# Attention with 64-wide values: values as the stationary operand, outputs born turned

## The chip, the cores and the metric

The kernel runs on one core of a Trainium2 chip. It is one program for the whole forward pass, and its time is the device time of one execution, in microseconds. The engines of the core are TensorE (PE in the rows; PEld are its weight loads), VectorE (DVE), ScalarE (ACT), GpSimd (POOL) and SyncE (SP), which issues most DMAs. Each has its own queue, worked in order; they meet only through semaphores.

## The reference

Two layers of one kind (latent attention, mLSTM and SSD mixers, then routed experts) are followed by two layers of a second kind. Only these second layers are changed. Each computes, for 512 tokens of width 1024:

```python
h = rms_norm(x, attn_norm_g[l])
proj = h @ w_in[l]
(mq, mk, mv, dq, dk, dv, sq, sk, sv, iq, ik, iw) = jnp.split(proj, offsets, axis=-1)
moba = moba_attention(...)          # 4 heads, values 64 wide
...
a = probs(q1, k1) - lam * probs(q2, k2)         # differential: 4 heads, values 128 wide
diff = rms_norm(diff, diff_subln_g[l]) * (1.0 - lam_init)
dsa = dsa_attention(...)            # 4 heads, values 64 wide, top 128 keys by the indexer
mix = jnp.concatenate([merge_heads(moba), merge_heads(diff), merge_heads(dsa)], axis=-1)
x = x + mix @ w_out[l]
h2 = rms_norm(x, ffn_norm_g[l])
x = x + (jax.nn.silu(h2 @ w_gate[l]) * (h2 @ w_up[l])) @ w_down[l]
```

All three attentions are causal softmaxes over tiles of 128 queries. The order of the rows of `w_out` and of the columns of `mix` may be chosen freely as long as both agree.

## The kernel before

A dense product with float32 accuracy is made of three matmuls: each operand is split into a high part (a copy rounded by ScalarE) and a low part (the difference, by VectorE or GpSimd), and `product` (lines 264 to 266) multiplies high by high, low by high and high by low. Weights come in units of 128x2048 through `WeightStream`: SyncE loads a unit into one of three raw slots, ScalarE makes its high part (L215), VectorE or GpSimd the low part (L253), and TensorE may use it once `lo_ready` has counted it. A raw slot is loaded anew when its low part is made. `split_hi_half` and `split_lo_half` do half a unit at a time; the first layers' attention (`mla_attention_stage`) uses them.

A second layer goes through these stages, each a block that ends with a barrier of all engines:

1. Projection, with the search for the top keys (`IndexSearch`) beside it.
2. `transpose_stage` "qk_t": queries and keys are turned to head-major form, 16 chunks.
3. `pair_attention_stage`: 32 pairs in a software pipeline written out by hand. A pair is two heads and one tile of 128 queries; with t = 0 to 3 it sees 128, 256, 384 or 512 keys. Pairs 0 to 15 are differential, 16 to 23 of moba, 24 to 31 of dsa; I call the last sixteen plain. In step i TensorE does the scores of pair i (L3351, masks L3354), turns the probabilities of pair i-2 (L3367) and multiplies those of pair i-3 with the values (L3380). VectorE takes the maxima of pair i (L3393); for a differential pair it then merges the two heads (L3399 to L3402), in steps chosen by `search.step` it does a round of the search (L2977, L2978), and for a plain pair i-4 it divides and stores the output (L3411, L3414). ScalarE copies the turned probabilities of pair i-2 (L3434), makes the exponentials of pair i (L3442), stores the differential outputs (L3425), and from step 20 on sums their squares (`DiffEnd`, L3292); GpSimd then multiplies them by the inverse norm (L3282, four instructions).
4. `transpose_stage` "y2_t": all eight column blocks of the output are turned (L300, 32 transposes), copied as high parts by ScalarE (L314) and split by VectorE (L328, L330, where the differential gain is multiplied in). GpSimd makes the low part of the first unit of `w_out` beside it.
5. `out_ffn_stage`: for each token tile t and column half c, 8 blocks of `mix` against four units of `w_out` (24 matmuls of 512 columns), added to x by VectorE (`add`, L2278). When a tile's two halves are added, ScalarE squares it (L2179) and takes the root, VectorE normalises it (L2285), and TensorE turns it (`turn`, L2090) for the feed-forward product, which follows in the same block.

In stage 5 the turning of tile t stands in TensorE's queue after the first half of tile t+1:

```python
                        last.then_inc(summed, 1)
                        if c == 0 and t >= 1:
                            turn(t - 1)
```

For a plain pair the probabilities are the stationary operand of L3380 and the 64 columns of values move, twice, so the output has the queries on partitions and the two heads side by side. The turning of a plain pair waits only for its exponentials:

```python
                        if pairs[j]["merge"]:
                            pe.wait_ge(merged, merges[j])
                        else:
                            pe.wait_ge(exp_done, 2 * j + 2)
```

Of the kernel before, what the change touches and what calls it, by code (L numbers as in the profile page):

```python
# [514 lines left out]
def by_head(ap, heads):  # L515
    return ap.rearrange("p (h c) -> p h c", h=heads)
# [1332 lines left out]
Y_SLOTS = (2, 10)  # L1849
PRODUCT_BANKS = (6, 7, 0, 1, 4, 5, 2, 3)  # L1850
# [4 lines left out]
def out_ffn_stage(env, stage, first, first_ffn, yt, xo, x, gains, small, out, saved):  # L1855
# [17 lines left out]
             "stored", "tile_summed")  # L1873
    (gains_loaded, small_loaded, summed, added, squared, root_ready, root_inverted, normed, turned, x_hi, x_lo, s_made, s_hi,
     s_lo, w_made, w_hi_done, w_lo_dve, w_lo_pool, p_done, p1_kept, gated_left, gated_right, combined,
     hidden_done, hidden_hi, hidden_lo, stored, tile_summed) = (env.sem(stage, n) for n in names)
# [23 lines left out]
    with ExitStack() as local:  # L1900
# [71 lines left out]
        def sum_bank(t, c):  # L1972
            return ps[:, 2 * (t % 2) + c, :]

# [59 lines left out]
        with nc.Block() as block:  # L2034
# [45 lines left out]
            def _(pe):  # L2080
# [50 lines left out]

                for t in range(T):
                    for c in range(2):
                        if t >= 2:
                            pe.wait_ge(added, 2 * (t - 2) + c + 1)
                        for kp in range(2):
                            u = 2 * c + kp
                            w_hi, w_lo = stream.ready(pe, first + u)
                            for j in range(4):
                                k = 4 * kp + j  # L2140
                                a = tuple(y[:, k, t * P:(t + 1) * P] for y in yt)
                                last = product(nc, sum_bank(t, c), a, (w_hi[:, j], w_lo[:, j]), k == 0, k == KD - 1)
                        last.then_inc(summed, 1)
                        if c == 0 and t >= 1:
                            turn(t - 1)
# [28 lines left out]
            def _(act):  # L2174
# [43 lines left out]
                for u in range(OUT):  # L2218
                    stream.split_hi(act, first + u)
# [52 lines left out]
            def _(dve):  # L2272
# [88 lines left out]
                for u in range(OUT):  # L2361
                    stream.split_lo(v, first + u)
# [596 lines left out]
class IndexSearch:  # L2959
# [5 lines left out]
    def __init__(self, env, ctx, proj):  # L2965
# [3 lines left out]
        self.masks = ctx.enter_context(env.nc.sbuf_tensor("index_masks", [P, T, S], F32R, allow_name_mangling=True))  # L2969
        self.masked = env.sem("index", "masked")  # L2970

    def mask(self, t):
        return self.masks[:, t, 0:(t + 1) * P], self.tiles.index(t) + 1
# [50 lines left out]
def second_layer_units(base=0):  # L3024
# [3 lines left out]
    units += weight_units("w_out_2", D, 0, D)  # L3028
# [276 lines left out]
def pair_attention_stage(env, stage, pairs, lam, search, diff_end, prefetch):  # L3305
# [10 lines left out]
    names = ("scores_ready", "max_ready", "exp_done", "merged", "turned", "turned_copied", "out_ready", "out_stored",  # L3316
             "vector_step")
    (scores_ready, max_ready, exp_done, merged, turned, turned_copied, out_ready, out_stored,
     step) = (env.sem(stage, n) for n in names)
    banks = [(j, h) for j, u in enumerate(pairs) for h in range(1 if u["merge"] else 2)]  # L3320
    first_bank = [banks.index((j, 0)) for j in range(N)]
    after_bank = first_bank[1:] + [len(banks)]
    merges = [sum(u["merge"] for u in pairs[:j + 1]) for j in range(N)]

    with ExitStack() as local:
# [8 lines left out]

        with nc.Block() as block:
            @block.sync
            def _(sp):
                env.stream.load(sp, prefetch)

            @block.tensor  # L3340
            def _(pe):
                for i in range(N + 3):
# [27 lines left out]
                    if i >= 3:  # L3370
# [4 lines left out]
                        if j >= 2:  # L3375
                            pe.wait_ge(out_stored, j - 1)
                        for h, v in enumerate(u["v"]):
                            w = v[0].shape[1]
                            for b in range(nb):
                                last = nc.tensor.matmul(ps[:, 6 + j % 2, h * w:(h + 1) * w],  # L3380
                                                        prob_t[:, (first_bank[j] + h) % 4, b * P:(b + 1) * P], v[b],
                                                        start=(b == 0), stop=(b == nb - 1))
# [3 lines left out]
            def _(dve):  # L3386
                v = nc.vector
                link = Link(dve, step)
                for i in range(N + 4):
# [5 lines left out]
                    if 1 <= i < N + 1 and pairs[i - 1]["merge"]:  # L3395
# [4 lines left out]
                        link(v.scalar_tensor_tensor(out=ratio[:, j:j + 1], in0=recip[:, j, 1:2], scalar=total[:, j, 0:1],  # L3400
                                                    in1=lam, op0=ALU.mult, op1=ALU.mult))
                        v.scalar_tensor_tensor(out=prob[:, j % 3, 0, 0:nk], in0=prob[:, j % 3, 1, 0:nk],  # L3402
                                               scalar=ratio[:, j:j + 1], in1=prob[:, j % 3, 0, 0:nk], op0=ALU.mult, op1=ALU.add
                                               ).then_inc(merged, 1)
                    search.step(dve, link, i)
                    if i >= 4:
                        j = i - 4
                        u = pairs[j]
                        if not u["merge"]:
                            dve.wait_ge(exp_done, 2 * j + 2)  # L3410
                            link(v.reciprocal(recip[:, j, :], total[:, j, :]))  # L3411
                            dve.wait_ge(out_ready, j + 1)
                            dve.wait_ge(out_stored, j)
# [266 lines left out]
```

## Time and profile before

| | us |
|---|---|
| median of 3 runs | 2554.39 (2551.23 to 2559.26) |
| profiled execution | 2554.73 |
| its span, first to last instruction | 2552.7 |
| TensorE busy | 2377.1 (93%) |
| VectorE busy | 1737.8 (68%) |
| ScalarE busy | 1323.1 (52%) |
| GpSimd busy | 605.5 (24%) |
| attention stage of the second layers (layer 0, layer 1) | 1359.28 to 1448.87, 2054.38 to 2141.92 |
| output product and what hangs on it | 1456.00 to 1505.76, 2149.04 to 2198.76 |

The times of the lower rows are counted from the start of the span. The stage table cuts the attention stage at VectorE's maxima: that of pair 16 begins at 1399.50 (2092.54), of pair 26 at 1425.87 (2118.90), of pair 31 at 1441.12 (2134.16). Busy times of different engines overlap; a piece is bound by an engine that is busy in nearly all of it. PEclk 1.00 is TensorE at 2.4 GHz, 0.50 at 1.2 GHz.

### The profile page before, as it was taken

What the parts mean: (1) busy time and instruction counts of PE and PEld (TensorE: products, weight loads), DVE (VectorE), ACT (ScalarE), POOL (GpSimd) and SP (SyncE); (2) the same over time, 40 slices, a digit from 0 to 9 for tenths busy, and PEclk for the clock granted to TensorE, in tenths of its full rate; (3) what the DMA queues carried; (4) which work ended last, traced back from release to release, by engine and by line L of the source; (5) the groups of instructions that cost most, each with busy time, mean ns of one, the idle gap of its engine ahead of it and who ended that gap; (6) DMA issues with size and microseconds to landing.
All of it is one profiled execution on the core that took longest, in us unless ns stands there. A gap on an engine that the chain in (4) does not pass through costs nothing. (4 is left out here: it accounts for less than half of the span.)

```text
span 2552.7 us, 37194 instructions
## 1 busy us (share of the span) xinstructions
PE 2377.1 (93%) x14216; PEld 1998.1 (78%) x14216; DVE 1737.8 (68%) x2737; ACT 1323.1 (52%) x2658; POOL 605.5 (24%) x335
## 2 busy tenths in 40 slices
PE   7999987987999987987998999999999989999999
PEld 7866776777866776766786789998887867899987
DVE  1755767873755757876698569994256984799942
ACT  3447616763557616765756744443157476444431
POOL 2401305771401305772450110000034501100000
PEclk9999988998999988998998999999999999999999
DMA  4210028983210018983120113223232202033221
GB/s 163 75 47 18 1 84 331 356 317 123 75 46 18 1 51 345 354 306 125 67 100 1 35 79 116 100 96 112 70 104 72 83 1 91 34 118 115 100 83 66
DMA packets 54993, 285.83 MB, mean 112 GB/s; under 512 B 13216, under 2 KB 13216, under 8 KB 28704
## 3 DMA queue, kind: packets, MB, share of 16 engines
q1 hardware_dynamic: 45600, 266.65, 29.1%
q0 software_dynamic: 9216, 16.80, 1.7%
q8 instruction: 114, 1.87, 0.3%
q14 instruction: 63, 0.52, 0.1%
HBM read 275.02 MB, written 25.17 MB: 118 GB/s over the span
## 5 line engine op out<-in xcount | busy, mean ns | idle before, releaser
L253 POOL TENSOR_TENSOR weights_lo<-weights_raw,weights_hi 128x2048 fp32r<-128x2048 f32 (+4 forms) x51 | 230.3, 4517 | 725.7 <-issue 358.5
L264 PE MATMUL ps<-x_operands,weights_hi 128*128 128x256 f32 x1232 | 349.0, 283 | 5.7 <-DVE weights_lo L2026 5.1
L266 PE MATMUL ps<-x_operands,weights_lo 128*128 128x256 f32 x1232 | 348.4, 283 | 0.0
L265 PE MATMUL ps<-x_operands,weights_hi 128*128 128x256 f32 x1232 | 345.9, 281 | 0.0
L215 ACT ACTIVATE weights_hi<-weights_raw 128x2048 fp32r<-128x2048 f32 (+5 forms) x82 | 140.6, 1714 | 305.0 <-PE ps L266 287.6
L264 PEld LDWEIGHTS ps<-x_operands,weights_hi 128*128 128x128 f32 x1232 | 231.8, 188 | 8.4 <-DVE weights_lo L2026 6.8
L265 PEld LDWEIGHTS ps<-x_operands,weights_hi 128*128 128x128 f32 x1232 | 233.6, 190 | 0.0
L266 PEld LDWEIGHTS ps<-x_operands,weights_lo 128*128 128x128 f32 x1232 | 230.6, 187 | 0.0
L264 PE MATMUL ps<-weights_hi,attn_ht_hi 128*128 128x512 f32 (+2 forms) x576 | 203.8, 354 | 5.0 <-DVE weights_lo L253 2.2
L265 PE MATMUL ps<-weights_lo,attn_ht_hi 128*128 128x512 f32 (+2 forms) x576 | 200.7, 348 | 0.0
L266 PE MATMUL ps<-weights_hi,attn_ht_lo 128*128 128x512 f32 (+2 forms) x576 | 199.9, 347 | 0.0
L253 DVE TENSOR_TENSOR weights_lo<-weights_raw,weights_hi 128x2048 fp32r<-128x2048 f32 (+3 forms) x31 | 60.5, 1952 | 173.3 <-ACT weights_hi L215 173.3
L264 PE MATMUL ps<-weights_hi,x_operands 128*128 128x512 f32 x384 | 152.9, 398 | 6.3 <-PEq L287 6.2
L265 PE MATMUL ps<-weights_lo,x_operands 128*128 128x512 f32 x384 | 152.4, 397 | 0.0
L264 PE MATMUL ps<-weights_hi,xt_hi 128*128 128x480 f32 (+2 forms) x384 | 138.2, 360 | 6.1 <-DVE weights_lo L253 2.5
L2020 ACT ACTIVATE weights_hi<-ffn_w_sums 128x1024 fp32r<-128x1024 f32 x66 | 70.0, 1060 | 133.6 <-DVE ffn_w_sums L2330 133.6
L266 PE MATMUL ps<-weights_hi,xt_lo 128*128 128x480 f32 (+2 forms) x384 | 135.4, 353 | 0.0
L265 PE MATMUL ps<-weights_lo,xt_hi 128*128 128x480 f32 (+2 forms) x384 | 134.9, 351 | 0.0
L264 PEld LDWEIGHTS ps<-weights_hi,attn_ht_hi 128*128 128x128 f32 x576 | 109.2, 190 | 28.8 <-issue 9.1
L266 PE MATMUL ps<-weights_hi,ffn_hidden_lo 128*128 128x512 f32 x320 | 125.8, 393 | 0.0
L266 PEld LDWEIGHTS ps<-weights_hi,attn_ht_lo 128*128 128x128 f32 x576 | 109.4, 190 | 13.5
L265 PEld LDWEIGHTS ps<-weights_lo,attn_ht_hi 128*128 128x128 f32 x576 | 109.3, 190 | 11.7
(522 smaller groups left out, 6238.8 us busy)
## 6 DMA issues: line engine op xcount, KB each, us to landing
weights_raw<-in_stream SPq DMA_DIRECT2D x96, 1024.0 KB, 4.8
weights_raw<-in_expert_gu SPq DMA_DIRECT2D x34, 1024.0 KB, 9.3
expert_raw<-in_expert_gu SPq DMA_DIRECT2D x30, 1024.0 KB, 9.3
expert_raw<-in_expert_down SPq DMA_DIRECT2D x18, 1024.0 KB, 8.0
weights_raw<-in_expert_down SPq DMA_DIRECT2D x14, 1024.0 KB, 8.1
weights_raw<-in_stream SPq DMA_DIRECT2D x12, 960.0 KB, 4.7
ffn_raw<-in_stream SPq DMA_DIRECT2D x10, 1024.0 KB, 5.0
weights_raw<-in_stream SPq DMA_DIRECT2D x8, 700.0 KB, 9.8
```

The lines of the kernel that those rows point to most:

```text
L215: self.nc.scalar.activation(self.split_tiles(u)[0][:, 0:n], self.env.raw[:, u % self.RAW, 0:n], ACT.Copy).then_inc(self.hi_ready, 1)
L253: eng.tensor_tensor(lo[:, 0:n], self.env.raw[:, u % self.RAW, 0:n], hi[:, 0:n].bitcast(F32), ALU.subtract).then_inc(self.lo_ready, 1)
L264: nc.tensor.matmul(out, a[0], b[0], start=start, stop=False, **more)
L265: nc.tensor.matmul(out, a[0], b[1], start=False, stop=False, **more)
L266: return nc.tensor.matmul(out, a[1], b[0], start=False, stop=stop, **more)
L2020: nc.scalar.activation(ring(g)[0], quarter(c, w_of[p]), ACT.Copy).then_inc(w_hi_done, 1)
```

## The change

Four things change in each second layer.

- The plain pairs. VectorE scales their probabilities by the reciprocal sum before they are turned (two TENSOR_SCALARs; `weighed` counts it, and TensorE waits for it). The values are now the stationary operand, 64 columns of them for each head, and the turned probabilities move: head 0 goes to the output's partitions 0 to 63, head 1 to 64 to 127, so the output has its columns on partitions. Four tiles fill one bank; then ScalarE copies the bank as high part and VectorE subtracts for the low part, straight into the operand `plain_yt` of the output product. The divide-and-store on VectorE is gone.
- The splits of the first two units of the output weights move into the attention stage: ScalarE in steps 9 and 13, VectorE in steps 20, 21, 24 and 25, half a unit each. SyncE loads all four units from there.
- Stage 4 is gone. The four differential blocks are turned at the start of stage 5 (16 transposes into banks 4 to 7) and split there.
- The order of the output product. The rows of `w_out` are stored so that the plain blocks come first, and units go by row half first. The first half product (plain) of tiles 0 and 1 runs ahead, four times 12 matmuls; then each tile gets its second half (differential). `turn(t-1)` stands after the second half of column half 0.

The chunks of the turned queries and keys are reordered so that `plain_yt` lies where the differential ones were, and a gap tile fixes the place.

```diff
+                for k in range(NDIFF):
+                    for t in range(T):
+                        last = nc.tensor.transpose(diff_bank(k)[:, t * P:(t + 1) * P], diff[0][:, t, k * P:(k + 1) * P], ident)
+                    last.then_inc(diff_turned, 1)
+                for t in range(2):
+                    for c in range(2):
+                        half(0, t, c)
+                pe.wait_ge(diff_lo, NDIFF)
                 for t in range(T):
+                    for c in range(2 if t >= 2 else 0):
+                        pe.wait_ge(added, 2 * (t - 2) + c + 1)
+                        half(0, t, c)
                     for c in range(2):
...
+                        half(1, t, c).then_inc(summed, 1)
                         if c == 0 and t >= 1:
                             turn(t - 1)
...
-                        if pairs[j]["merge"]:
-                            pe.wait_ge(merged, merges[j])
-                        else:
-                            pe.wait_ge(exp_done, 2 * j + 2)
+                        pe.wait_ge(weighed, j + 1)
...
+                            for b in range(nb):
+                                for h in range(2):
+                                    last = nc.tensor.matmul(turned_out(m)[h * HD:(h + 1) * HD, t * P:(t + 1) * P], u["v"][h][b],
+                                                            prob_t[:, (first_bank[j] + h) % 4, b * P:(b + 1) * P],
+                                                            start=(b == 0), stop=(b == nb - 1))
...
+                        else:
+                            for h in range(2):
+                                last = v.tensor_scalar(prob[:, j % 3, h, 0:nk], prob[:, j % 3, h, 0:nk], recip[:, j, h:h + 1],
+                                                       None, ALU.mult)
+                        last.then_inc(weighed, 1)
                     search.step(dve, link, i)
...
+                    if i in lo_at:
+                        u, half = lo_at[i]
+                        env.stream.split_lo_half(v, first_out + u, half)
+                    if last_of(i - 4):
+                        m = (i - 4 - M) // T
+                        dve.wait_ge(hi_stored, m + 1)
+                        v.tensor_tensor(yt[:, 1, m, :], turned_out(m), yt[:, 0, m, :].bitcast(F32), ALU.subtract
+                                        ).then_inc(lo_stored, 1)
```

VectorE's queue in step 20 of the attention stage, before (`attn_top` are the maxima, MAX and MATCH_REPLACE a round of the search, `attn_recip` the reciprocals):

```order
L3393 TENSOR_REDUCE attn_top<-ps 128x2
L2977 MAX index_top<-proj_12305 128x8
L2978 MATCH_REPLACE proj_12305<-index_top,proj_12305 128x256
L3411 RECIPROCAL attn_recip<-attn_total 128x2
L3414 TENSOR_TENSOR proj_12305<-ps,attn_recip 128x128
L3393 TENSOR_REDUCE attn_top<-ps 128x2
```

The same step and the next maximum in the changed kernel:

```order
L3432 TENSOR_REDUCE attn_top<-ps 128x2
L3438 RECIPROCAL attn_recip<-attn_total 128x2
L3447 TENSOR_SCALAR attn_prob<-attn_prob,attn_recip 128x512 x2
L3002 MAX index_top<-proj_12305 128x8
L3003 MATCH_REPLACE proj_12305<-index_top,proj_12305 128x256
L237 TENSOR_TENSOR weights_lo<-weights_raw,weights_hi 128x1024
L3432 TENSOR_REDUCE attn_top<-ps 128x2
```

The scaling of the pair before and half a low part now stand between two maxima, and the store is gone.

TensorE's queue from the last pairs into the output product, before (`attn_prob_t` are the turned probabilities, `x_operands` the turned outputs):

```order
L3367 MATMUL ps<-consts,attn_prob 128x128 x8
L3380 MATMUL ps<-proj_12305,attn_prob_t 128x64 x14
L3335 UNCONDITIONAL_BRANCH
L288 UNCONDITIONAL_BRANCH
L300 MATMUL ps<-consts,proj_12305 128x128 x32
L287 UNCONDITIONAL_BRANCH
L2079 UNCONDITIONAL_BRANCH
L264 MATMUL ps<-weights_hi,x_operands 128x512
```

And in the changed kernel:

```order
L3397 MATMUL ps<-consts,attn_prob 128x128 x8
L3419 MATMUL ps<-attn_prob_t,proj_12305 64x128 x14
L3368 UNCONDITIONAL_BRANCH
L2086 UNCONDITIONAL_BRANCH
L2149 MATMUL ps<-consts,proj_12305 128x128 x16
L264 MATMUL ps<-weights_hi,plain_yt 128x512
L265 MATMUL ps<-weights_lo,plain_yt 128x512
```

One block boundary and half of the transposes have left the place between attention and the output product.

## Rows read from the trace of the kernel before

**Rows 1.** Stage table: stretch, length, busy us and instructions of each engine, PEclk, DMA

```profile
1359.28:1399.50 40.22, 36.53 (x197) 24.05 (x197) 33.92 (x85) 26.62 (x90) 0.00 (x0) 0.84 0.00 1
1399.50:1425.87 26.37, 25.94 (x191) 20.49 (x192) 20.06 (x52) 23.94 (x95) 1.01 (x2) 1.00 0.01 2
1425.87:1441.12 15.25, 15.18 (x110) 11.95 (x109) 6.07 (x16) 10.62 (x35) 3.02 (x4) 1.00 0.01 2
1441.12:1448.87 7.75, 6.80 (x58) 6.28 (x56) 3.03 (x11) 3.96 (x10) 0.00 (x0) 1.00 0.00 0
1448.87:1456.00 7.13, 3.69 (x33) 3.51 (x33) 5.12 (x8) 4.38 (x8) 4.55 (x1) 1.00 0.17 47
1456.00:1505.76 49.76, 49.38 (x216) 39.29 (x217) 25.13 (x23) 18.94 (x25) 6.72 (x4) 0.97 0.30 117
2054.38:2092.54 38.16, 34.06 (x197) 22.07 (x197) 33.84 (x86) 26.45 (x90) 0.00 (x0) 0.91 0.00 1
```

**Rows 2.** Groups by form, VectorE, 1399.50 to 1429.68: busy, mean ns | idle before

```profile
L3414 DVE TENSOR_TENSOR proj<-ps,attn_recip 128x128 f32<-128x128 f32 x7 | 2.0, 291 | 0.2
L3411 DVE RECIPROCAL attn_recip<-attn_total 128x2 f32<-128x2 f32 x7 | 1.1, 160 | 0.1
...
L3006 DVE TENSOR_SCALAR index_masks<-proj 128x512 fp32r<-128x512 f32 x1 | 0.4, 421 | 0.0
...
L3006 DVE TENSOR_SCALAR index_masks<-proj 128x256 fp32r<-128x256 f32 x1 | 0.3, 283 | 0.0
```

**Rows 3.** Timeline (start, us, instructions), first layers' attention stage, from 189 us

```profile
189.55 1.09 PE L1149 MATMUL ps<-mla_prob_t,y 128*64 128x128 f32 x16
...
189.98 0.88 DVE L1169 TENSOR_SCALAR mla_prob<-mla_prob,mla_recip 128x512 f32<-128x512 f32 x2
...
190.58 1.13 PE L1124 MATMUL ps<-shared 64*128 64x512 f32 x4
...
191.52 1.07 ACT L225 ACTIVATE weights_hi<-weights_raw 128x1024 fp32r<-128x1024 f32 x1
...
194.94 1.22 DVE L237 TENSOR_TENSOR weights_lo<-weights_raw,weights_hi 128x1024 fp32r<-128x1024 f32 x1
```

**Rows 4.** Timeline, end of that stage: high and low part of a turned output

```profile
234.42 0.60 ACT L1203 ACTIVATE yt_mla_hi<-ps 128x512 fp32r<-128x512 f32 x1 [1.26 <-PE ps L1149]
235.05 0.69 DVE L1178 TENSOR_TENSOR yt_mla_lo<-ps,yt_mla_hi 128x512 fp32r<-128x512 f32 x1 [3.72 <-ACT yt_mla_hi L1203]
```

**Rows 5.** Timeline, TensorE, last plain pairs and start of the output product

```profile
1437.46 1.90 PE L3380 MATMUL ps<-proj,attn_prob_t 128*128 128x64 f32 x16
...
1439.29 1.13 PE L3351 MATMUL ps<-qk_t 64*128 64x512 f32 x4
...
1458.78 0.63 PE L264 MATMUL ps<-weights_hi,x_operands 128*128 128x512 f32 x1
...
1461.36 0.39 PE L264 MATMUL ps<-weights_hi,x_operands 128*128 128x512 f32 x1
```

**Rows 6.** Timeline, from tile 0's last add to its turning

```profile
1469.25 0.69 DVE L2278 TENSOR_TENSOR x<-x,ps 128x512 f32<-128x512 f32 x1 [3.97 <-PE ps L266]
...
1472.96 1.28 DVE L2285 SCALAR_TENSOR_TENSOR ffn_h<-x,ffn_rs,ffn_g 128x1024 f32<-128x1024 f32 x1
...
1474.65 1.03 PE L2090 MATMUL ps<-consts,ffn_h 128*128 128x128 f32 x8
```

**Rows 7.** Timeline, GpSimd and VectorE on SBUF operands, from 1484 us

```profile
1484.58 1.62 POOL L2265 TENSOR_TENSOR x_operands<-ffn_parts,x_operands 128x512 fp32r<-128x512 f32 x1 [30.86 <-ACT ffn_parts L2188]
...
1484.96 2.32 DVE L2330 TENSOR_TENSOR ffn_w_sums<-weights_raw 128x1024 f32<-128x1024 f32 x1
...
1489.54 1.23 DVE L2330 TENSOR_TENSOR ffn_w_sums<-weights_raw 128x1024 f32<-128x1024 f32 x1
```

**Rows 8.** Stage table, two slices of 5 us among the differential pairs

```profile
1385.00:1390.00 5.00, 3.77 (x21) 2.48 (x20) 4.57 (x12) 3.65 (x12) 0.00 (x0) 0.92 0.02 5
1390.00:1395.00 5.00, 5.00 (x28) 3.46 (x28) 3.89 (x11) 3.04 (x12) 0.00 (x0) 0.74 0.00 0
```

More of the change, by code:

```diff
@@ L1852, with out_ffn_stage @@
 X_OF = {"P1": "A11", "P2": "A12", "P3": "S4", "P4": "A22", "P5": "S1", "P6": "S2", "P7": "S3"}
-def out_ffn_stage(env, stage, first, first_ffn, yt, xo, x, gains, small, out, saved):
+def out_ffn_stage(env, stage, first, first_ffn, yt, diff, xo, x, gains, small, out, saved):
     nc, ps, ident, stream = env.nc, env.ps, env.ident, env.stream
@@ L2130, in multiply, with half @@
                     last.then_inc(p_done, 1)
+                def half(kp, t, c):
+                    w_hi, w_lo = stream.ready(pe, first + 2 * kp + c)
+                    for j in range(4):
+                        k = 4 * kp + j
+                        a = tuple(y[:, t * P:(t + 1) * P] for y in yt[k])
+                        last = product(nc, sum_bank(t, c), a, (w_hi[:, j], w_lo[:, j]), k == 0, k == KD - 1)
+                    return last
+                for k in range(NDIFF):
[6 more added lines that the diff above has]
+                pe.wait_ge(diff_lo, NDIFF)
                 for t in range(T):
+                    for c in range(2 if t >= 2 else 0):
+                        pe.wait_ge(added, 2 * (t - 2) + c + 1)
+                        half(0, t, c)
                     for c in range(2):
[L2134 to L2143, printed above, removed]
+                        half(1, t, c).then_inc(summed, 1)
                         if c == 0 and t >= 1:
@@ L2359, in after @@
                         v.tensor_tensor(hidden(c, 1), hidden(c, 1), by_f(q), ALU.mult).then_inc(hidden_done, 1)
-                for u in range(OUT):
+                for k in range(NDIFF):
+                    dve.wait_ge(diff_hi, k + 1)
+                    v.scalar_tensor_tensor(out=yt[4 + k][1], in0=diff_bank(k), scalar=diff[1], in1=yt[4 + k][0].bitcast(F32),
+                                           op0=ALU.mult, op1=ALU.subtract).then_inc(diff_lo, 1)
+                for u in range(2, OUT):
                     stream.split_lo(v, first + u)
@@ L3027, in second_layer_units @@
     first_out = base + len(units)
-    units += weight_units("w_out_2", D, 0, D)
+    units += [("out_2", r, r + 4 * P, c, c + BANK) for r in range(0, D, 4 * P) for c in range(0, D, BANK)]
     first_ffn = base + len(units)
@@ L3333, in score, with turned_out, last_of @@
             return ps[:, 2 * (i % 2) + h, 0:pairs[i]["nk"]]
+        def turned_out(m):
+            return ps[:, 6 + m % 2, :]
+        def last_of(j):
+            return 0 <= j and not pairs[j]["merge"] and (j - M) % T == T - 1
         with nc.Block() as block:
@@ L3394, in _ @@
                                         ).then_inc(max_ready, 1)
-                    if 1 <= i < N + 1 and pairs[i - 1]["merge"]:
+                    if 1 <= i < N + 1:
                         j = i - 1
@@ L3399, in _ @@
                         link(v.reciprocal(recip[:, j, :], total[:, j, :]))
[L3400 to L3404, printed above, removed]
@@ L3419, in _ @@
             def _(act):
-                for i in range(N + 2):
+                for i in range(N + 4):
                     if i >= 4 and pairs[i - 4]["merge"]:
```

113 lines of the change are left out of this document (68 added, 45 removed).

## The prediction

> **What bounds the kernel now.** I read the table of stages first, then the engines' instructions inside the stage that changes, then the seam behind it, then a stage of the same kernel that already does what the change does.
>
> The stage table [rows 1] gives the attention stage of the second layers in pieces, for both layers. Pairs 0 to 15 (the differential pairs) take 40.22 us in the first layer and 38.16 us in the second. From VectorE's maximum of pair 16 to that of pair 26 (plain pairs, with the index search still running) TensorE is busy for 25.94 of 26.37 us and VectorE for only 20.06. From pair 26 to pair 31 TensorE has 15.18 of 15.25 us, VectorE 6.07. So the plain pairs are bound by TensorE, and VectorE has room: 6.31 us in the first of the two pieces. Then the chain through the last pair, 7.75 us, and the seam: 7.13 us of which TensorE works 3.69. The output product and what hangs on it take 49.76 us with TensorE busy throughout. All of this occurs twice. The chip is one core, and these pieces lie one behind the other, so what they gain or lose is gained or lost by the kernel.
>
> **The change part by part, for one layer.**
>
> *The matmul of a plain pair.* At 512 keys it is 16 records; they start at 1437.46 and the next scores at 1439.29, so 1.83 us [rows 5]. The first layers' attention already has the new form, 128x64 stationary on column halves and 128 columns moving: 16 records from 189.55 to 190.58, 1.03 us [rows 3]. The records of the two halves evidently overlap. I take 0.8 us off a 512-key pair, and in proportion off the others, about 2 us off four pairs, 8 us off TensorE in a layer. Against it stands the change of shape around these matmuls. The 1.03 us of those rows were measured with such a change on both sides, so the row has the price in it. The Trainium skill (TensorEngine Tiling (Array Packing), Key Properties) says that a change of the tiling mode drains TensorE, which speaks against alternating shapes in every pair; the row cannot separate the drain, and a sum without the rule would be the same.
>
> *VectorE's new work.* Each plain pair is now scaled before it is turned: a reciprocal and two TENSOR_SCALARs over all keys. At 512 keys two of them take 0.88 us [rows 3] and hold the engine for about 0.80, since the next instruction starts before the last has ended. The same operation at 256 keys is 283 ns against 421 at 512 [rows 2], 69 ns for 128 keys; so 0.66, 0.52 and 0.38 us for the smaller pairs. The store from PSUM goes (0.29 us a piece [rows 2], 0.21 us of the engine), and the reciprocal (0.16 [rows 2], 0.19 with its wait) moves up by three pairs. Four halves of the weights' low parts come in (steps 20, 21, 24, 25), 1.22 us each [rows 3], 1.14 of the engine. One low part of a turned output, 0.69 us [rows 4], 0.60 of the engine, falls into the piece. For pairs 16 to 26: nine scalings 5.10, three reciprocals more 0.57, four halves 4.56, one output 0.60, less six stores 1.26: +9.57 us. VectorE goes from 20.06 to 29.6 us, and the piece was 26.37 us long. The room of 6.31 us does not hold it, so VectorE takes TensorE's place as the bound: at least 29.6 - 26.37 = +3.3 us. Laying each engine's rows one behind another by the waits of the code, I find 0.6 to 1.4 us in which VectorE still waits (the first maximum, and the root of the differential norm). I take **+4.4 us**. TensorE's gain is spent waiting here: the turning of pair i-2 now stands behind its scaling, and behind this wait are queued the product of pair i-3 and the scores of pair i+1, for which VectorE's next maximum waits in turn.
>
> *Pairs 26 to 31.* VectorE's 6.07 us become some 10 and still fit in 15.25. TensorE has about 1.4 us less to do, but maximum, exponentials, scaling, turning and copy of a pair now follow one another on three engines; laid out, that gives the 15.2 us again. I take **0**, bounds -1.4 and +1.
>
> *The tail.* Behind the last maximum the chain gets the scaling (0.80 and a reciprocal 0.19), loses about 1.4 us of the last two pairs' products, loses the store, and gets ScalarE's copy and VectorE's low part, 0.60 and 0.69 us [rows 4], one behind the other: 7.75 becomes about 9.4, **+1.65 us**, bounds 1.0 and 2.2.
>
> *ScalarE.* It gets two halves of a high part at steps 9 and 13, among the differential pairs, 1.07 us each [rows 3], where it is busy 26.62 of 40.22 us [rows 1]; it waits for maxima there. I cost them at nothing; without this cover they would cost 2.1 us. Four turned outputs (0.60 us [rows 4]) stand where ScalarE waits for VectorE anyway.
>
> *The seam and the output product.* Before, the stage between them turns all eight column blocks (32 transposes, which are the 3.69 us of TensorE), waits for the splits, and crosses another barrier: 7.13 us from the last store to the first product [rows 1]. Now 16 transposes remain, 1.85 us, behind one barrier of 0.3 us, and the first products need only what attention has already split: 2.15 us, a gain of 5.0. While the first four half products run (48 matmuls of 0.23 us, 11.1 us), ScalarE and VectorE split the four differential blocks (some 4.2 us) and then the two later units, whose low part is ready 7.3 us after the start of the stage; the cover is ample. GpSimd loses the 4.55 us of a low part, which nobody waited for.
>
> But the order has a price. The turning of the first normalised tile, turn(0), waits for this tile's sum, square, root and scaling: from the add at 1469.25 to the end of the normalisation at 1474.24 and the turning at 1474.65 are 5.4 us, of which the product of 24 matmuls (5.5 us) hid everything [rows 6]. After the change only 12 matmuls, 2.77 us, stand between the tile's last product and turn(0). So TensorE waits about 2.4 us. The later tiles have 36 matmuls there and lose nothing. The four-tile tail behind it moves VectorE's last add by 0.9 us, which the two first products of the feed-forward hide. From attention's end to the feed-forward's first product: 0.3 + 1.85 + 192 x 0.2305 + 3 x 0.92 + 2.4 + 0.3 = 51.9 us against 7.13 + 49.76 = 56.9: **-5.0 us**. In it the clock is taken as full. Before, it fell after the seam: matmuls of 0.63 us at 1458.78 in place of 0.39 at 1461.36 [rows 5], seven of them, 1.4 us lost. If that fall stays, the gain is 3.6. I take -4.2.
>
> *GpSimd against VectorE.* GpSimd's four multiplications of the differential norm (4.03 us, in rows 1 as 1.01 and 3.02) now meet scalings of pairs 25 and 26, where before they met only reads of PSUM. An elementwise VectorE instruction took 2.32 us while GpSimd worked and 1.23 without it [rows 7]; doubling 1.2 us of scalings costs at most 1.2. I take +0.5. The Trainium skill (SBUF — State Buffer, Who interferes with whom) says more: TENSOR_SCALAR in its two-port mode and GpSimd exclude one another for a whole instruction. Rows 7 agree that the two disturb each other; what the rule would make of it is the third rival.
>
> **Sum.** A layer: 4.4 + 0 + 1.65 + 0.5 - 4.2 = +2.35; twice: +4.7. The profiled execution took 2554.73 us (span 2552.7), 0.34 above the median of 2554.39, so nothing is corrected: 2559.4, rounded to **2559.5 us**, 0.2% more.
>
> **The rivals.**
>
> *The clock falls among the plain pairs* (slower). TensorE's busy share there falls from 98% to about 75% (25.94 less some 3 of about 31 us). Among the differential pairs it was the same, 3.77 of 5 us, before the clock went from 2.4 GHz towards 1.2 (granted 0.74 in the next 5 us) [rows 8], in the first layer alone: that layer's piece is 2.06 us longer [rows 1]. It decides from two such falls a layer, 4.1 us, with the fall behind the seam kept: 4.4 + 1.65 + 0.5 + 4.1 - 3.6 = +7.05, twice +14: 2569. For it: the lower share. Against it: the second layer kept its clock among its differential pairs (0.91 over a piece whose start is slow in both). 0.25.
>
> *VectorE's work hides better* (level or a little faster): no waits left in the piece (+3.3), pairs 26 to 31 gain 1.4, the tail costs 1.0, no clock fall behind the seam (-5.0): -2.1 a layer, 2550.5. Against it: the order of VectorE's queue, in which a half of 1.14 us stands ahead of a maximum. 0.17.
>
> *GpSimd locks VectorE out.* Each of the four scalings of pairs 25 and 26 waits for one GpSimd instruction of 1.0 us: +4 in place of +0.5, some 1.5 of it in VectorE's waits: +2 a layer, 2563.5. 0.10. This is the rule just cited.
>
> *The halves do not overlap in this stage.* The product stays at 1.83 us and TensorE, with the scaling's wait ahead of it, is the bound again: about +4 a layer, 2567.5. Rows 3 speak against it: the same form, three engines as busy. 0.03.
>
> **How the numbers follow.** The forecast has 0.45. A measurement of this kernel tells about 0.3% from no change, here 7.7 us: faster means under 2547, slower over 2562.4. The first, third and fourth rival lie above (0.38), and a tenth of the forecast's chance too, while a fifth of the first rival is a single fall and stays within: slower 0.38. Within: 0.55. Only the second rival at its far end, with a longer gain in the output product, is faster: 0.07. The range goes from the second rival to the first: 2550 to 2569.
>
> **What would show it.** In the changed kernel's stage table the piece from pair 16 to pair 26 should be about 31 us with VectorE busy in nearly all of it and TensorE waiting for the scaling; pairs 26 to 31 about 15.2; the tail about 9.4. The first product should start about 2.2 us after attention's end, and TensorE should wait some 2.4 us before turn(0), once a layer. A plain pair's 16 records should take about 1.1 us. The prediction is wrong if the first piece keeps its 26 us, if the granted clock there is under 0.95, or if TensorE waits for a differential split.

## Result and profile after

The changed kernel took 2563.13 us, median of 5 runs (2561.64 to 2571.19), beside 2554.39 for the kernel before: ratio 1.0039, interval 1.0021 to 1.0057. Run once more later it took 2563.61, ratio 1.0038, 1.0024 to 1.0051. It is slower by 0.4%: 8.7 us where 4.7 were forecast. That is inside the range, and just outside the 0.3% within which 0.55 of the chances lay.

There are two profiles of it: one of a run of 2571.19 us (span 2569.4), one of 2559.88 (span 2558.1). First the stage table of the first layer in the earlier one. Cut as in [rows 1]: pair 16 to pair 26, pair 26 to 31, the tail to the end of attention, the seam to the first product, and the output product to the feed-forward's first. Columns: stretch, length, then busy us and instructions of PE, PEld, DVE, ACT and POOL, then PEclk and DMA (share, GB/s).

```profile
1403.88:1435.14 31.26, 27.43 (x191) 18.41 (x191) 29.36 (x72) 25.21 (x96) 0.42 (x1) 0.89 0.10 35
1435.14:1450.44 15.30, 13.64 (x110) 8.48 (x109) 10.06 (x21) 10.61 (x36) 3.65 (x4) 1.00 0.01 2
1450.44:1461.11 10.67, 6.57 (x58) 5.18 (x56) 4.38 (x9) 5.14 (x12) 0.00 (x0) 0.84 0.00 0
1461.11:1463.13 2.02, 1.69 (x16) 1.72 (x17) 0.31 (x2) 1.03 (x2) 0.00 (x0) 1.00 0.33 126
1463.13:1515.27 52.14, 49.52 (x219) 39.67 (x218) 24.47 (x25) 18.41 (x27) 6.73 (x4) 0.97 0.24 93
```

The same stretches in the later profile, first layer:

```profile
1397.14:1429.61 32.47, 27.44 (x191) 18.59 (x191) 29.44 (x72) 26.07 (x97) 1.26 (x2) 0.89 0.10 34
1429.61:1444.17 14.56, 13.58 (x110) 8.46 (x109) 9.75 (x21) 10.13 (x35) 2.82 (x3) 1.00 0.01 2
1444.17:1453.43 9.26, 5.16 (x58) 3.76 (x56) 4.38 (x9) 5.04 (x12) 0.00 (x0) 1.00 0.00 0
1453.43:1455.45 2.02, 1.69 (x16) 1.72 (x17) 0.31 (x2) 1.03 (x2) 0.00 (x0) 1.00 0.33 126
1455.45:1507.56 52.11, 49.52 (x219) 39.61 (x218) 24.44 (x25) 18.42 (x27) 6.74 (x4) 0.97 0.24 93
```

VectorE has taken TensorE's place from pair 16 to 26: 29.4 us busy, where it had 20.06, and the piece is 30.7 to 32.5 us long in the four layers instead of 26.37. What one profile has more there the other has more behind pair 26: together 46.56 and 47.03, against 41.62 before. From pair 16 to 26 TensorE now waits for the scaling, 3.6 us in all in the first layer of the earlier profile, and its turnings behind two of these waits are slow (0.87 us is the rule for six at 2.4 GHz):

```profile
1414.28 1.49 PE L3397 MATMUL ps<-consts,attn_prob 128*128 128x128 f32 x6 [1.42 <-DVE attn_prob L3447]
1427.91 1.46 PE L3397 MATMUL ps<-consts,attn_prob 128*128 128x128 f32 x6 [1.69 <-DVE attn_prob L3447]
```

The seam has shrunk from 7.13 to 2.02 us, but the output product has grown from 49.76 to 52.1. From pair 16 on a layer costs 4.2 us more in the later profile (110.42 against 106.26) and 5.1 in the earlier, where the tail too ran at a granted clock of 0.84.

The rest of the difference between the two profiles lies ahead of pair 16. The earlier one comes to its first maximum 3.2 us later (1363.67 against 1360.50); from 1175 to 1200 us its granted clock was 0.93, in the other 1.00. And pairs 0 to 15 took between 36.2 and 40.2 us in the four layers of these two executions of one kernel (38.77 and 37.01 before): the shortest had a granted clock of 0.95, the longest 0.79, by how long the stage began at 1.2 GHz and by whether the clock fell again near its end.

Three places in the rows. A plain pair's product, 16 records, TensorE:

```profile
1421.41 1.09 PE L3419 MATMUL ps<-attn_prob_t,proj 128*64 128x128 f32 x16
1422.43 1.13 PE L3384 MATMUL ps<-qk_t 64*128 64x512 f32 x4
```

The next scores start 1.02 us after it, in place of 1.83 [rows 5]: the halves overlap. The Trainium skill (TensorEngine Tiling (Array Packing), Key Properties) says that a change of the tiling mode drains TensorE. There is such a change on both sides of these records, and both are in the 1.02, so no run here shows the drain as a cost of its own.

The tail in the earlier profile, and then in the later one (TensorE, last two pairs: turnings, products):

```profile
1452.58 0.87 PE L3397 MATMUL ps<-consts,attn_prob 128*128 128x128 f32 x6 [1.37 <-DVE attn_prob L3447]
1455.40 1.97 PE L3397 MATMUL ps<-consts,attn_prob 128*128 128x128 f32 x8 [1.36 <-DVE attn_prob L3447]
1457.31 2.44 PE L3419 MATMUL ps<-attn_prob_t,proj 128*64 128x128 f32 x28
```

```profile
1446.31 0.88 PE L3397 MATMUL ps<-consts,attn_prob 128*128 128x128 f32 x6 [1.36 <-DVE attn_prob L3447]
1449.14 1.09 PE L3397 MATMUL ps<-consts,attn_prob 128*128 128x128 f32 x8 [1.37 <-DVE attn_prob L3447]
1450.16 1.90 PE L3419 MATMUL ps<-attn_prob_t,proj 128*64 128x128 f32 x28
```

The waits for the scaling are the same. Only in the first does the clock stand at 1.2 GHz behind the second wait: 1.97 for 1.09, 2.44 for 1.90, 1.4 us of tail.

And the turning of the first normalised tile, TensorE, earlier profile:

```profile
1482.62 0.39 PE L266 MATMUL ps<-ffn_out_w_hi,x_operands 128*128 128x512 f32 x1
1485.30 1.29 PE L2097 MATMUL ps<-consts,ffn_h 128*128 128x128 f32 x8 [2.29 <-DVE ffn_h L2305]
1486.82 0.63 PE L265 MATMUL ps<-ffn_out_w_lo,x_operands 128*128 128x512 f32 x1
1487.24 0.63 PE L266 MATMUL ps<-ffn_out_w_hi,x_operands 128*128 128x512 f32 x1
...
1488.95 0.63 PE L264 MATMUL ps<-ffn_out_w_hi,x_operands 128*128 128x512 f32 x1
1489.38 0.44 PE L265 MATMUL ps<-ffn_out_w_lo,x_operands 128*128 128x512 f32 x1
```

The forecast wait stands there, 2.29 us, and behind it what had not been forecast: the clock at 1.2 GHz, matmuls of 0.63 us where 0.40 is the rule. It is so in both layers of both profiles.

### The profile page after: what moved, and what is told of

The parts are those of the page before. It is cut to its first block and busy times, and to the rows that moved or that the text cites. A ratio compares the mean times of both kernels' runs of the same rounds, so it can differ in the third digit from the quotient of the medians.

```text
span 2569.4 us, 37074 instructions
## 1 busy us (share of the span) xinstructions
PE 2378.9 (93%) x14184; PEld 1990.3 (77%) x14184; DVE 1758.8 (68%) x2775; ACT 1323.0 (51%) x2660; POOL 596.3 (23%) x333
## 5 line engine op out<-in xcount | busy, mean ns | idle before, releaser
L253 POOL TENSOR_TENSOR weights_lo<-weights_raw,weights_hi 128x2048 fp32r<-128x2048 f32 (+4 forms) x49 | 221.2, 4515 | 688.2 <-issue 359.4
L215 ACT ACTIVATE weights_hi<-weights_raw 128x2048 fp32r<-128x2048 f32 (+4 forms) x80 | 136.8, 1710 | 301.6 <-PE ps L266 288.1
L265 PE MATMUL ps<-weights_lo,x_operands 128*128 128x512 f32 x320 | 126.3, 395 | 0.0
L264 PE MATMUL ps<-weights_hi,x_operands 128*128 128x512 f32 x320 | 126.0, 394 | 0.0
```

What stands on the lines that cost most here:

```text
L215: self.nc.scalar.activation(self.split_tiles(u)[0][:, 0:n], self.env.raw[:, u % self.RAW, 0:n], ACT.Copy).then_inc(self.hi_ready, 1)
L253: eng.tensor_tensor(lo[:, 0:n], self.env.raw[:, u % self.RAW, 0:n], hi[:, 0:n].bitcast(F32), ALU.subtract).then_inc(self.lo_ready, 1)
L264: nc.tensor.matmul(out, a[0], b[0], start=start, stop=False, **more)
L265: nc.tensor.matmul(out, a[0], b[1], start=False, stop=False, **more)
```

## Experiments

The theory to be tested: VectorE's total bounds the plain pairs; TensorE's new waits cost what they last, and where TensorE is the bound also the clock behind them. The rivals: the scaling as a step of each pair's chain, not VectorE's total; falls of the clock that come whatever TensorE does; GpSimd's hold on VectorE.

**The changed kernel once more** (after_again).

> The changed kernel once more, for a second profile beside its variants. Theory: the two layers add some +13 us in any profile (first layer 145.0 to 151.6, second 143.2 to 150.0 in the first profile), and the other 3 us of that profile lie in stages that the change does not touch (longer stretches at 1.2 GHz); so about 2563. If the further 3 us belong to the change: about 2569 again, at the same places.

2563.61 us (2559.88 to 2565.97). Its profile has the layers at 147.06 and 146.61 us against 145.03 and 143.23. The theory's +13 was too much: with pairs 0 to 15 left out the layers add 2 x 4.2 = 8.4, close to the median's 8.7.

**The low parts' halves behind the last scaling** (lo_late).

```
-    lo_at = {20: (0, 0), 21: (0, 1), 24: (1, 0), 25: (1, 1)}
+    lo_at = {33: ((0, 0), (0, 1)), 34: ((1, 0), (1, 1))}
```

> The four halves of the weights' low parts move from steps 20, 21, 24 and 25 to steps 33 and 34, behind the last scaling, where VectorE waits 5 us for the last output. Theory (VectorE's sum bounds the piece from pair 16 to 26, and the halves are what put it over): VectorE 29.4 - 4.6 = 24.8 us there, TensorE bounds again with some waits, the piece goes from 31.0 to about 27, the two waits for x6 transposings of 1.4 and 1.7 us go and with them the falls of the clock there; tail unchanged; -4 a layer, -8 in all against the changed kernel, about 2555. Rival (the scaling as a step of each pair's chain makes the waits, not VectorE's sum): the piece stays at 29.5 or more, -3 in all. Rival (nothing to do with VectorE; the new matmul form and the clock): no change.

2561.5 us: 2 gained, not 8, and the two intervals (1.0015 to 1.0041 of the kernel before, 1.0024 to 1.0051 for the changed kernel) overlap. From pair 16 on the profile has 108.96 us a layer, 1.5 less than the changed kernel's later one. Its stage table, from pair 16 to the first product:

```profile
1396.78:1425.97 29.19, 25.86 (x191) 17.43 (x191) 24.97 (x67) 24.44 (x96) 0.83 (x1) 0.94 0.01 1
1425.97:1441.54 15.57, 13.42 (x110) 8.53 (x109) 9.21 (x21) 11.45 (x36) 3.20 (x4) 1.00 0.01 2
1441.54:1451.59 10.05, 5.16 (x58) 3.77 (x56) 8.83 (x13) 5.03 (x12) 0.00 (x0) 1.00 0.18 57
1451.59:1455.14 3.55, 3.23 (x17) 3.26 (x17) 1.28 (x2) 1.77 (x3) 0.00 (x0) 0.52 0.80 282
```

The first piece lost 1.5 to 3.3 us (in the two profiles of the changed kernel it takes 30.7 to 32.5) for 4.4 us of VectorE's work, and then neither VectorE (24.97) nor TensorE (25.86) fills it. The theory had about 27, the rival of the pair's chain 29.5 or more: the piece came nearer to the rival, so VectorE's sum alone does not set it. Most of this was given back: four halves are 4.62 us, the last low part came 0.8 us late, and the clock fell across the seam, 1.5 us. In return the clock did not fall behind the first turning, though TensorE waits 2.29 us there too:

```profile
1477.32 1.09 PE L2097 MATMUL ps<-consts,ffn_h 128*128 128x128 f32 x8 [2.29 <-DVE ffn_h L2305]
1478.17 0.48 PE L264 MATMUL ps<-ffn_out_w_hi,x_operands 128*128 128x512 f32 x1
1478.49 0.40 PE L265 MATMUL ps<-ffn_out_w_lo,x_operands 128*128 128x512 f32 x1
```

**The first turning later** (turn0_late).

```
-                        if c == 0 and t >= 1:
+                        if c == (t == 1) and t >= 1:
                             turn(t - 1)
```

> TensorE's turning of the first normalised tile goes behind the tile's second column block: 24 matmuls (5.5 us) instead of 12 (2.8 us) stand ahead of it. Theory: the wait of 2.3 us goes, and since TensorE no longer stands idle the clock does not fall behind it (six matmuls of 0.63 us instead of 0.40, 1.2 us): -3.5 a layer, -7 in all against the changed kernel, about 2556. Rival (the fall comes at that place anyway, the wait only precedes it): -2.3 a layer, -4.6 in all. Rival (later turning delays the splits of the tile and so the first product of the feed-forward): nothing gained.

2555.58 us, 8.0 less than the changed kernel, level with the kernel before (1.0003, 0.9994 to 1.0012). TensorE at the first turning:

```profile
1477.78 0.39 PE L266 MATMUL ps<-ffn_out_w_hi,x_operands 128*128 128x512 f32 x1
1478.01 1.03 PE L2097 MATMUL ps<-consts,ffn_h 128*128 128x128 f32 x8
1478.80 0.48 PE L264 MATMUL ps<-weights_hi,plain_yt 128*128 128x512 f32 x1
1479.12 0.40 PE L265 MATMUL ps<-weights_lo,plain_yt 128*128 128x512 f32 x1
```

No wait, no slow matmuls: the product takes 48.08 instead of 52.14, 4.05 us a layer, of which the wait is 2.3 and the clock the rest. The rival with the fall at that place anyway (-4.6) is out. The granted clock is 1.00 over the product in both layers, so the fall that stood behind the seam before [rows 5] has gone as well.

**Work for TensorE in its waits** (fill; 18 more of these turnings stand ahead of the first tile's turning).

```
+                        if i in FILL:
+                            pe.wait_ge(turned_copied, first_bank[j] - 1)
+                        for _ in range(FILL.get(i, 0)):
+                            nc.tensor.transpose(ps[:, 4 + first_bank[j] % 2, 0:P], ident, ident)
                         pe.wait_ge(weighed, j + 1)
```

> The changed kernel with turnings of the identity that nobody reads where TensorE waits: 11 ahead of each of the waits at steps 20, 24, 32 and 33 (into the bank that the step's own turnings fill next), 18 ahead of the turning of the first normalised tile. No wait is taken away. Theory (the clock falls because TensorE stands idle there): granted clock 1.00 in the last piece of the attention stage (0.84 before) and behind the first tile's turning; x8 turnings of the last pair 0.93 us instead of 1.97; the tail 9.4 instead of 10.6, the output product 1.2 us shorter, the piece from pair 16 to 26 about 0.5 shorter (VectorE bounds it): -2.5 to -3 a layer, about -5 in all, 2558. Rival (the falls come by a pattern of their own): clock as before and no gain, or +1 for the added turnings.

2558.98 us (1.0016, 1.0007 to 1.0025), 4.6 less with no wait taken away. The table, first layer:

```profile
1392.81:1423.48 30.67, 27.67 (x215) 18.98 (x215) 29.25 (x72) 24.62 (x96) 0.00 (x0) 1.00 0.10 36
1423.48:1439.37 15.89, 13.49 (x109) 8.44 (x109) 9.98 (x22) 11.23 (x36) 4.08 (x4) 1.00 0.01 2
1439.37:1448.63 9.26, 7.84 (x80) 6.12 (x78) 4.39 (x9) 5.04 (x12) 0.00 (x0) 1.00 0.00 0
1448.63:1450.65 2.02, 1.70 (x17) 1.73 (x17) 0.31 (x1) 1.03 (x2) 0.00 (x0) 1.00 0.33 99
1450.65:1501.20 50.55, 49.89 (x237) 40.44 (x236) 24.47 (x25) 18.41 (x27) 6.74 (x4) 1.00 0.25 97
```

From pair 16 on the granted clock is 1.00 in every piece of both layers, where both profiles of the changed kernel had 0.89 from pair 16 to 26 and 0.97 over the product: it is TensorE's standing idle that brings the falls. And here they have a price only where TensorE is late. The output product gains 1.6 us and the tail is 9.26 in both layers; pairs 16 to 31 take 46.56 us with the clock at 1.00, as in the earlier profile with 0.89.

**The halves in two places, with the later turning** (lo_mixed).

```
+    lo_at = {29: ((0, 0),), 33: ((0, 1), (1, 0)), 34: ((1, 1),)}
```

> The kernel with the later first turning (turn0_late), and the four halves of the low parts at step 29 (one, where VectorE waits 2.2 us for scores) and behind the last scaling (three, 3.4 us, which end ahead of the last output's high part; with four, in lo_late, the last low part came 0.9 us late and the clock fell across the seam). Theory (the halves are what puts VectorE over in the piece from pair 16 to 26, and lo_late lost its gain again at the tail and the seam): that piece 29.2 as in lo_late, tail 9.3, seam 2.0, output product 48.1: -2 a layer, -4 in all against turn0_late's 2555.6, about 2551.5. Rival (the gain of that piece is lost again wherever the halves go, since TensorE then waits for scalings): no gain, 2555.5.

2549.41 us: ratio to the kernel before 0.9975, 0.9966 to 0.9984. The gain of the piece is not lost again if the halves fit where VectorE is idle. The table, first layer, from pair 16 to the first product, and then the first piece of the second layer:

```profile
1399.45:1427.72 28.27, 24.48 (x191) 16.51 (x191) 25.00 (x68) 24.31 (x96) 0.84 (x1) 1.00 0.01 1
1427.72:1443.31 15.59, 13.42 (x110) 8.54 (x109) 10.35 (x23) 11.47 (x36) 3.19 (x4) 1.00 0.01 2
1443.31:1452.57 9.26, 5.16 (x58) 3.76 (x56) 7.78 (x12) 5.04 (x12) 0.00 (x0) 1.00 0.24 73
1452.57:1454.58 2.01, 1.69 (x16) 1.72 (x17) 0.30 (x1) 1.02 (x2) 0.00 (x0) 1.00 0.78 314
```

```profile
2090.85:2120.02 29.17, 25.82 (x191) 17.46 (x191) 25.00 (x68) 24.47 (x96) 0.83 (x1) 0.94 0.00 1
```

At a clock of 0.94 the piece takes 0.9 us more, with the same work: now that VectorE no longer fills it, a fall of the clock costs something here too.

**Each head turned when it is scaled** (per_head), with the later turning.

```
+                            pe.wait_ge(weighed, g + 1)
```

> The kernel with the later first turning (turn0_late), and TensorE turns the first head of a plain pair as soon as that head is scaled, not when both are. Theory (VectorE's sum bounds the piece from pair 16 to 26; behind it each pair's chain bounds): there no more than -0.3, in pairs 26 to 31 and the tail 0.3 to 0.4 us for each of the two or three waits of some 1.4 us, so -1 a layer, 2553.5. Rival (the scaling as a step of the chain makes the waits in the first piece too): -2 us there as well, -3 a layer, 2549.5.

2553.03 us, 2.5 less than with the later turning alone (0.9982 to 1.0003 of the kernel before, against 0.9994 to 1.0012: the intervals overlap). The tail is 8.85 in place of 9.25 where the clock held (10.15 in the other layer, at 0.83), pairs 16 to 31 46.17 and 46.47 in place of 46.57 and 47.16. The piece from pair 16 to 26 is 0.3 us shorter in both layers (30.92 and 32.31 for 31.21 and 32.60). So about what the theory said, not the rival's -3 a layer: in the bound piece it changes little.

**The differential norm's multiplications on VectorE** (dve_mult), with the later turning (the same four TENSOR_TENSORs).

```
+        for t in {29: (0, 1), 30: (2,), 31: (3,)}.get(i, ()):
+            y = by_head(self.y[:, t, :], self.NH)
+            self.env.nc.vector.tensor_tensor(y, y, per_tile(self.ss[:, t, :], self.W), ALU.mult)
```

> The kernel with the later first turning (turn0_late), and the four multiplications of the differential norm on VectorE (128x512 on SBUF, about 0.65 us each: two at step 29, one at 30, one at 31, where it waits for scores) instead of GpSimd. Theory (GpSimd's four and VectorE's scaling of pair 26 hold each other up: two scalings of 256 keys took 1.9 to 2.2 us beside GpSimd, 0.62 without): the two scalings 0.62 again, pairs 16 to 31 shorter by 1.3 to 1.5 us, so -2.7 in all, 2553. Rival (that wait is hidden behind TensorE's work of those steps, or VectorE's own four cost as much): no change, 2555.5.

2560.2 us, 4.6 more. VectorE's first scaling of 256 keys behind the maximum of pair 26, in the changed kernel beside GpSimd and here without it (it is that of pair 25, not of pair 26 as the theory calls it, since step i scales pair i-1):

```profile
1434.72 4.08 POOL L3307 TENSOR_TENSOR proj<-proj,diff_ss 128x512 f32<-128x512 f32 x4 [95.40 <-DVE diff_ss L3327]
1436.73 2.22 DVE L3447 TENSOR_SCALAR attn_prob<-attn_prob,attn_recip 128x256 f32<-128x256 f32 x2
```

```profile
1431.52 0.62 DVE L3448 TENSOR_SCALAR attn_prob<-attn_prob,attn_recip 128x256 f32<-128x256 f32 x2
1448.78 0.68 DVE L3328 TENSOR_TENSOR proj<-proj,diff_ss 128x512 f32<-128x512 f32 x1
1449.57 0.88 DVE L3448 TENSOR_SCALAR attn_prob<-attn_prob,attn_recip 128x512 f32<-128x512 f32 x2
```

The hold is real, 1.6 us, but pairs 16 to 31 took 46.99 and 46.09 us against 46.57 and 47.16: 0.3 in the mean, less than the layers differ among themselves. VectorE got four multiplications in its place, so the run shows what the exchange is worth and not what the hold alone costs. The loss is elsewhere: the fourth multiplication stands ahead of the last scaling, the tails took 10.80 and 11.08 at clocks of 0.83 and 0.85 (10.73 and 9.25 without), and one seam 3.36 at 0.54. From pair 16 on the two layers of the profile lose 2.6 us together; where the other 2 of the 4.6 lie is open.

**Without the scaling** (no_scale), in the changed kernel:

```
-                            for h in range(2):
-                                last = v.tensor_scalar(prob[:, j % 3, h, 0:nk], ..., recip[:, j, h:h + 1], None, ALU.mult)
+                            last = v.reciprocal(recip[:, j, :], total[:, j, :])
```

> The changed kernel without the scaling of the plain pairs: their reciprocals are still taken, but the two TENSOR_SCALARs over the exponentials are left out, so the outputs of these pairs are not divided by their sums. Theory: VectorE loses 5.1 us of 29.4 from pair 16 to 26, and the step between exponentials and turning goes: that piece 31.0 (32.5 at the lower clock) to about 26.5, bounded by both engines, no waits above 1 us there; the tail 9.3 to 7.5; -6 a layer, about 2551. Rival (the halves of the low parts alone make the waits): that piece stays above 29.

2549.57 us, 14.0 less than the changed kernel. From pair 16 on, first layer:

```profile
1398.25:1424.41 26.16, 24.14 (x190) 16.29 (x190) 23.38 (x54) 23.66 (x95) 0.39 (x1) 1.00 0.12 42
1424.41:1439.52 15.11, 13.56 (x110) 8.62 (x110) 5.29 (x11) 11.88 (x37) 3.65 (x4) 1.00 0.01 2
1439.52:1447.86 8.34, 5.16 (x58) 3.77 (x56) 2.75 (x5) 5.04 (x12) 0.00 (x0) 1.00 0.00 0
```

The theory had 26.5 and 7.5 for the first and third. With the four halves still in place the first piece is as long as before the change. So it takes both, halves and scaling, to make VectorE the bound. And TensorE has 24.1 us to do where it had 25.94, but the piece is only 0.2 us shorter than before: no engine fills it any more (VectorE 23.38, ScalarE 23.66). What the faster product would be worth without scaling and without halves no run shows.

**The three orders together**, without (both) and with (both_fill) the work in the waits:

```
+    FILL = {20: 8, 24: 8, 32: 8, 33: 8}
```

> The three orders that gained, together: the first turning later (turn0_late), the four halves at steps 29, 33 and 34 (lo_mixed), each head turned as soon as it is scaled (per_head). Theory (the gains are of different places and add): lo_mixed's 2549.4, less 0.4 to 0.9 us a layer of waits for the second head: 2548. Rival (with the halves gone from VectorE's queue nothing waits for the second head): 2549.4 as in lo_mixed.

> The same kernel with 8 turnings of the identity that nobody reads ahead of the waits at steps 20, 24, 32 and 33. Theory (what is left over from run to run in the pieces from pair 16 on are falls of the clock behind these waits, up to 1.3 us in the tail and 0.9 in the piece from pair 16 to 26): granted clock 1.00 in all of these pieces of both layers, 0 to 2 us less than without, 2547. Rival (the order alone has already taken away the waits that the clock falls for): the same time.

2550.97 us (0.9984, 0.9972 to 0.9997) and 2548.89 (0.9981, 0.9972 to 0.9991). From pair 16 on a layer took 103.0 without and 102.4 with the filling, against 106.2 before and 103.2 and 104.1 in lo_mixed; the filled one, first layer, from pair 16 to the tail:

```profile
1398.57:1426.43 27.86, 26.44 (x206) 18.02 (x206) 24.98 (x68) 23.82 (x95) 0.44 (x1) 1.00 0.01 1
1426.43:1442.01 15.58, 13.67 (x110) 8.66 (x110) 10.34 (x23) 11.85 (x37) 3.60 (x4) 1.00 0.01 2
1442.01:1450.92 8.91, 7.12 (x74) 5.46 (x72) 7.69 (x12) 5.04 (x12) 0.00 (x0) 1.00 0.21 65
```

Inside the layers the gains add: at equal clocks in the first piece a layer takes 0.8 us less than lo_mixed's with the filling (1.00) and 1.1 less without (0.94). With the filling the clock holds at 1.00 in both layers from pair 16 on, as the theory had it. The times of these two and of lo_mixed cannot be told apart, so neither theory nor rival is decided by them: 1 us a layer is less than pairs 0 to 15 vary. All three beat both kernels.

## Why the prediction came out as it did

Per layer, from pair 16 on, in us:

| term | predicted | measured |
|---|---|---|
| pairs 16 to 31, GpSimd's part among it | +4.4 + 0 + 0.5 | +4.9 and +5.4 |
| tail | +1.65 | +1.5; +2.8 where the clock fell |
| seam and output product | -4.2 | -2.75 |
| sum | +2.35 | +4.2; +5.1 and +5.0 in the earlier profile |

**Right.** VectorE as the new bound, with the size: 29.6 us of work forecast, 29.4 measured; the filled kernel at full clock needs 30.67 for the piece, and the forecast was 30.8. Pairs 26 to 31 as they were, the tail (9.26 for 9.4), the seam with the first product (2.02 for 2.15), the wait ahead of the first turning (2.29 for 2.4), a plain pair's product (1.09 for 1.1). ScalarE's halves of a high part cost nothing that can be seen: at a granted clock of 0.85 pairs 0 to 15 took 38.78 us with them (second layer, earlier profile) and 38.77 without (first layer, before).

**Wrong: the size of the gain in the output product.** The step was "from attention's end to the feed-forward's first product ... 51.9 us", with "if that fall stays, the gain is 3.6" as its worst. Measured are 54.13. At full clock it is 52.57 (the filled kernel), 0.7 above that step: a matmul was priced at 0.2305 us, and the rows have one start every 0.2347 (96 in a row in turn0_late), which is 0.8 over 192 of them; the seam and the wait came 0.1 shorter each. The other 1.6 is the clock behind the wait, for which 0.8 had been set aside. The prediction took the fall of [rows 5] as something that the seam might or might not keep; it did not see that the wait which it had itself just forecast could bring one of its own. Turning later removes both, 4.05 us, and makes the change level with the kernel before. By the later profile the three terms missed by 1.45, 0.5 and -0.15 us a layer; twice their sum is 3.6, and 2559.5 with it 2563.1. That this meets the median so closely is in part luck: the execution behind that profile took 2559.88, with shorter pairs 0 to 15 than the kernel before had.

**The rivals.** The first, falls among the plain pairs, came true as an event and not as a price: the clock there is 0.89 in every layer of both profiles, by the prediction's own test ("under 0.95") a sign against it; but it was priced at 2.06 a fall, from pairs 0 to 15, where TensorE is busy for 35.08 of 38.77 us. That price also holds a slower start: 5 to 10 us behind the first maximum the granted clock was 0.70 in the first layer and 0.89 in the second. Here, where VectorE bounds, a fall cost 0 to 0.5 us: the filled kernel has 46.56 us at 1.00, the changed kernel 46.56 and 47.03 at 0.89. What the clock did cost was at the two places where TensorE is the last to finish, the tail and the product. The third rival, GpSimd's hold, has its 1.3 to 1.6 us of VectorE's time in the rows, and what it costs the kernel is not shown: the exchange in dve_mult was worth 0.3 us a layer in these pairs. The second and the fourth did not occur.

**Too simple.** That VectorE's work and a little waiting make the piece holds for the changed kernel alone. At a granted clock of 1.00 taking 4.3 us of VectorE's work out with the halves shortened it by 2.4 (30.67 to 28.27), and taking 5.9 out with the scaling by 4.5 (30.67 to 26.16). What then sets it, with TensorE, VectorE and ScalarE near 24 of 26 us, stays open: in lo_mixed's piece the waits that are left are TensorE's for VectorE (3.5 us) and ScalarE's for VectorE (3.5 us).

## What to carry to other kernels

Price a new wait of an engine whose clock depends on its work twice: for what it lasts, and for the work behind it at the lower clock, if that engine is the last to finish there; if another engine bounds the stretch, the second price is nothing, or nearly; where no engine fills it, there is one again (0.9 us in lo_mixed's piece at 0.94). Before a bound moves to another engine, look for what in that engine's queue can stand where it is idle later: the four halves cost some 2.5 us a layer from pair 16 to 31 in one place, and nothing that can be seen in another (lo_mixed's tail is 9.26 as without them). And when products are split so that work can begin earlier, count again what stands ahead of each consumer: 12 matmuls did not cover a chain that 24 had covered.

## Not expected of the hardware

The same wait does not always bring the same clock. Behind waits of 1.37 and 1.36 us in the tail the granted clock was 0.84 over that piece in both layers of one execution and 1.00 in both layers of another; turn0_late had one of each. Behind the 2.29 us ahead of the first turning it fell in all four, and in lo_late, with the same wait, in neither layer: there it had fallen at the seam just before. So the runs show that idle time brings the falls and that work in it prevents them, but not at which wait of several one will come. With turnings of the identity in these waits it fell in none, although TensorE's useful work was the same.

Of GpSimd and VectorE only one paid: four multiplications on GpSimd took 4.08 us beside the scalings and 4.03 before [rows 1], while two scalings of 256 keys took 2.22, 2.20 and 1.91 us in place of 0.62. The Trainium skill (SBUF — State Buffer, Who interferes with whom) says that when a VectorE instruction in a two-port mode meets one of GpSimd, the one which issues first keeps the shared ports for its whole instruction and the other is blocked. The rows agree as to who waits: GpSimd was at work when the scaling came (1434.72 and 1436.73). Which mode the scaling ran in they do not show.
